# Form units of the FFN input product: fifth tiles of two forms in one ring slot, sums in two portions, an earlier store of x, T4's product behind UA

## What is computed

```
x = x + 0.5 * swiglu_ffn(rmsnorm(x, ffn1_norm), ffn1_w_in, ffn1_w_out)
...
x = x + mixed @ w_out
x = x + 0.5 * swiglu_ffn(rmsnorm(x, ffn2_norm), ffn2_w_in, ffn2_w_out)

def swiglu_ffn(x, w_in, w_out):
    gate, up = jnp.split(x @ w_in, 2, axis=-1)
    return (jax.nn.silu(gate) * up) @ w_out
```

## Time and profile before

| what | us |
|---|---|
| median of 3 runs | 1813.66 (1813.22 to 1813.73) |
| the profiled execution | 1813.04 |
| its span, first to last instruction | 1811.2 |
| PE busy in it | 1759.3 |
| VectorE busy | 1467.6 |
| ScalarE busy | 1113.4 |
| one unit of width 512 (264.79 to 308.38) | 43.59 |

### The profile page before, as it was taken

How to read it: one execution, slowest core, us unless ns; L and a number is a source line. 1 busy time by engine, 2 the same in 40 slices (tenths; PEclk the granted TensorE clock), 3 DMA queues, 4 the chain that set the end, 5 groups by cost and what they waited for, 6 DMA issues and landing times.

```text
span 1811.2 us, 21336 instructions
## 1 busy us (share of the span) xinstructions
PE 1759.3 (97%) x7976; PEld 1449.1 (80%) x7976; DVE 1467.6 (81%) x1729; ACT 1113.4 (61%) x1461; POOL 100.1 (6%) x117
## 2 busy tenths in 40 slices
PE   9999999999999999999999999799999999999999
PEld 7777777777988888888888888677777777987887
DVE  7788888888999998575665555688888888899998
ACT  7566666666676666554454445466666666666664
POOL 0100000100000001100000000100000000000000
PEclk9999999999999999999999999899999999999999
DMA  9988888887754656555555445898888887765662
GB/s 380 299 259 260 250 253 255 249 244 195 281 194 160 239 209 202 184 183 180 163 182 167 163 163 209 296 258 246 253 259 259 248 259 226 220 224 196 227 225 96
DMA packets 169190, 408.30 MB, mean 225 GB/s; under 512 B 9112, under 2 KB 18352, under 8 KB 163584
## 3 DMA queue, kind: packets, MB, share of 16 engines
q1 hardware_dynamic: 154208, 342.03, 54.2%
q0 software_dynamic: 13760, 62.94, 15.9%
q10 hardware_dynamic: 1120, 1.97, 0.3%
HBM read 351.57 MB, written 5.79 MB: 197 GB/s over the span
## 4 chain that ended last, share of the span: by engine, by line
PE 76%; DVE 13%; issue 4%; DMA 3%; ACT 3%; SPq 1%; POOL 0%; ACTq 0%; DVEq 0%
PE bank L626 6%; PE bank L628 6%; PE bank L627 6%; DVE wlo L1300 6%; PE bank L685 5%; PE bank L687 5%; PE bank L686 5%; PE bank L757 5%; PE bank L759 5%; PE bank L758 5%; PE bank L669 5%; PE bank L670 5%; PE bank L671 5%; PE bank L783 3%; PE bank L785 3%
## 5 line engine op out<-in xcount | busy, mean ns | idle before, releaser
L1300 DVE TENSOR_TENSOR wlo<-raw,whi 128x1024 fp32r<-128x1024 f32 (+1 forms) x506 | 608.7, 1208 | 238.7 <-ACT whi L953 234.7
L953 ACT ACTIVATE whi<-raw 128x1024 fp32r<-128x1024 f32 (+1 forms) x506 | 530.0, 1049 | 340.0 <-PE bank L628 183.9
L685 PE MATMUL bank<-whi,xs 128*128 128x512 f32 (+1 forms) x608 | 239.2, 393 | 16.6 <-DVE wlo L1300 15.3
L687 PE MATMUL bank<-whi,xs 128*128 128x512 f32 (+1 forms) x608 | 234.7, 386 | 0.0
L686 PE MATMUL bank<-wlo,xs 128*128 128x512 f32 (+1 forms) x608 | 234.6, 386 | 0.0
L953 ACT ACTIVATE whi<-tsum 128x1024 fp32r<-128x1024 f32 (+1 forms) x120 | 120.4, 1034 | 72.8 <-DVE tmini L1467 38.3
L757 PE MATMUL bank<-whi,aw_hi 128*128 128x512 f32 x420 | 164.5, 392 | 0.0
L669 PE MATMUL bank<-whi,xs 128*128 128x512 f32 (+1 forms) x380 | 148.0, 390 | 16.9 <-DVE wlo L1300 16.9
L759 PE MATMUL bank<-whi,aw_lo 128*128 128x512 f32 x420 | 163.6, 389 | 0.0
L758 PE MATMUL bank<-wlo,aw_hi 128*128 128x512 f32 x420 | 163.4, 389 | 0.0
L626 PE MATMUL bank<-whi,xs 128*128 128x512 f32 x384 | 155.1, 404 | 0.4 <-DVE wlo L1300 0.4
(11 more groups left out here) (217 smaller groups left out, 3085.5 us busy)
## 6 DMA issues: line engine op xcount, KB each, us to landing
raw<-ffn_w_in SPq DMA_DIRECT2D x86, 1024.0 KB, 5.1
raw<-ffn_w_out SPq DMA_DIRECT2D x84, 1024.0 KB, 6.6
raw<-w_in SPq DMA_DIRECT2D x48, 1024.0 KB, 5.0
raw<-ffn_w_in SPq DMA_DIRECT2D x75, 512.0 KB, 4.8
tsum<-raw POOLq DMA_DIRECT2D x36, 1024.0 KB, 6.9
minis<-ffn_w_in SPq DMA_DIRECT2D x72, 256.0 KB, 5.2
last_plain<-ffn_w_in SPq DMA_DIRECT2D x36, 512.0 KB, 5.2
raw<-w_out SPq DMA_DIRECT2D x16, 1024.0 KB, 4.9
```

Of the source, the lines that this page charges most:

```text
L685: mm(banks[b][:, 0:w], xs[:, k + i, 0, tok], hi, start=starts[b] and k + i == 0, stop=False, skip_group_check=True)
L687: last = mm(banks[b][:, 0:w], xs[:, k + i, 1, tok], hi, start=False, stop=k + i == last_k, skip_group_check=True)
L953: A(whi[:, h % SLOTS, 0:n_el], src, ACT.Copy).then_inc(weights_hi, 1)
L1300: V.tensor_tensor(wlo[:, h % SLOTS, 0:n_el], src, whi[:, h % SLOTS, 0:n_el].bitcast(f32), ALU.subtract).then_inc(weights_lo, 1)
```

## The change

1. *Shared slots.* The fifth tiles of two forms lie in one ring half: T1 with B11 (`T1_B11`), T2 with B21 (`T2_B21`), T3 with B22 (`T3_B22`); T4's stays alone (`T4_LAST`). A unit has 24 halves. Since the shared half stands between the two forms' other halves, the order is now T1 (2), T1_B11, B11 (2), GA, GB, B21 (2), T2 (2), T2_B21, GC, T3 (2), T3_B22, B22 (2), UA, T4 (2), T4_LAST, UB, UC.
2. *Order.* B21 stands ahead of T2, GC ahead of T3, UA ahead of T4.
3. *Sums.* `sum_t1` and `sum_t3` have two portions of 1024 columns, the second with the fifth tile. sum_t1's stand before UB and before UC, sum_t3's before GB and before B21. sums_done counts four per unit.
4. *x.* The store to x_kept stands ahead of `x_power(2)`.

PE's matmuls are the same in number and size. The diff, cut to its core:

```diff
-T1, B11, GA, GB, T2, B21, T3, GC, B22, T4, UA, UB, UC = 0, 3, 6, 7, 8, 11, 14, 17, 18, 21, 24, 25, 26
-UNIT_HALVES = 27
+T1, T1_B11, B11, GA, GB, B21, T2, T2_B21, GC, T3, T3_B22, B22, T4, T4_LAST, UA, UB, UC = (
+    0, 2, 3, 5, 6, 7, 9, 11, 12, 13, 15, 16, 19, 21, 18, 22, 23)
+UNIT_HALVES = 24
...
-                        last = (B11 + 2, T3 + 2, B22 + 2, T4, GA, GB, GC, UA, UB, UC)[i]
+                        last = (B11 + 1, T3_B22, B22 + 1, T4, GA, GB, GC, UA, UB, UC)[i]
...
-            x_power(2)
             pool.wait_ge(x_updated, 8 * 2)
             pool.dma_start(x_kept.rearrange("(b p) d -> p b d", p=P), x[:]).then_inc(x_stored, 16)
+            x_power(2)
             for j in range(1, UNITS):
-                add_piece(1, j, "B22", T1, t2_added)
-                add_piece(1, j, "B21", T2, t4_added)
+                add_piece(1, j, "B22", T1_B11, t2_added)
+                add_piece(1, j, "B21", T2_B21, t4_added)
...
+            def last_tiles(h, w, *parts):
+                pe.wait_ge(weights_lo, h + 1)
+                for i, (bank_out, stationary, start, stop) in enumerate(parts):
+                    last = tile(h, i, bank_out, stationary, 4, w, start, stop)
+                last.then_inc(weights_used, 1)
...
+                form(base + T1, Z, s1, w, True, False)
+                last_tiles(base + T1_B11, w, (Z, s1, False, True), (Y, a11, True, False))
+                form(base + B11, Y, a11, w, False, True)
                 act_turn(u, j - 1)
                 pe.wait_ge(copied, 3 * first + 1)
                 plain(base + GA, 0, (Z, X), (False, True), w, -1)
                 plain(base + GB, 2, (Z, X), (False, True), w, -1)
+                form(base + B21, V, a12, w, True, False)
                 pe.wait_ge(copied, 3 * first + 2)
+                form(base + T2, Y, s2, w, False, False)
+                last_tiles(base + T2_B21, w, (Y, s2, False, True), (V, a12, False, True))
+                plain(base + GC, 4, (Z, X), (False, False), w, FORM_K0 - 1)
                 pe.wait_ge(copied, 3 * first + 3)
+                form(base + T3, Y, s3, w, False, False)
+                last_tiles(base + T3_B22, w, (Y, s3, False, True), (Z, s4, False, False))
+                form(base + B22, Z, s4, w, False, True)
                 pe.wait_ge(w_done, first + 1)
+                plain(base + UA, 0, (V, Y), (False, False), w, -1)
+                form(base + T4, Y, a22, w, False, False)
+                last_tiles(base + T4_LAST, w, (Y, a22, False, False))
+                for i in range(2):
+                    plain(base + UB + i, 2 + 2 * i, (V, Y), (False, False), w, FORM_K0 - 1)
...
+            def split_two(h, src0, src1, w):
+                dve.wait_ge(weights_hi, h + 1)
+                V.tensor_tensor(wlo[:, h % SLOTS, 0:w], src0, whi[:, h % SLOTS, 0:w].bitcast(f32), ALU.subtract)
+                V.tensor_tensor(wlo[:, h % SLOTS, w:2 * w], src1, whi[:, h % SLOTS, w:2 * w].bitcast(f32),
+                                ALU.subtract).then_inc(weights_lo, 1)
...
+            def sum_t1(u, j, i):
                 n11, n12, w = unit_piece(u, j, "B11"), unit_piece(u, j, "B12"), UNIT_W[j]
+                if i == 0:
+                    full(n11)
+                    full(n12)
+                    if j > 1:
+                        dve.wait_ge(weights_lo, unit_half(u, j - 1) + T4_LAST + 1)
+                done = V.tensor_tensor(t_half(i, w), form_half(n12, i, w), form_half(n11, i, w), ALU.add)
+                if i:
+                    done = V.tensor_tensor(tmini[:, 0:w], form_last(n12, w), form_last(n11, w), ALU.add)
+                done.then_inc(sums_done, 1)
```

More of the change, by code:

```diff
@@ L1091, in unit @@
                 first, w2 = (UNITS - 1) * u + j - 1, 2 * w
-                def form_split(form, i, name=None):
-                    src = form_half(unit_piece(u, j, name), i, w) if name else t_half(i, w)
-                    split(base + form + i, src, form_el(i, w))
+                n11, n12, n21, n22 = (unit_piece(u, j, name) for name in ("B11", "B12", "B21", "B22"))
                 def plain_split(name, half):
@@ new lines, in unit @@
+                split_two(base + T2_B21, tmini[:, 0:w], form_last(n21, w), w)
+                plain_split("GC", GC)
+                for i in range(2):
+                    act_e.wait_ge(sums_done, 4 * first + 3 + i)
+                    split(base + T3 + i, form_half(n12, i, w), w2)
+                act_e.wait_ge(weights_used, base + T2_B21 + 1)
+                A(gset[:, s, 0, 0:w], Y[:, 0:w], ACT.Copy).then_inc(copied, 1)
+                loaded(n22)
+                split_two(base + T3_B22, form_last(n12, w), form_last(n22, w), w)
@@ L1513, in unit @@
                 first, w2 = (UNITS - 1) * u + j - 1, 2 * w
-                def form_split(form, i, name=None):
-                    src = form_half(unit_piece(u, j, name), i, w) if name else t_half(i, w)
-                    split(base + form + i, src, form_el(i, w))
+                n11, n12, n21, n22 = (unit_piece(u, j, name) for name in ("B11", "B12", "B21", "B22"))
                 def plain_split(name, half):
                     split(base + half, plain_half(unit_piece(u, j, name), w2), w2)
-                for i in range(3):
-                    form_split(T1, i)
@@ L1524, in unit @@
-                form_split(B11, 0, "B11")
+                for i in range(2):
+                    split(base + T1 + i, t_half(i, w), w2)
+                split_two(base + T1_B11, tmini[:, 0:w], form_last(n11, w), w)
+                split(base + B11, form_half(n11, 0, w), w2)
                 swiglu(u, j - 1)
-                for i in range(1, 3):
-                    form_split(B11, i, "B11")
+                split(base + B11 + 1, form_half(n11, 1, w), w2)
                 plain_split("GA", GA)
-                sum_t3(u, j)
+                sum_t3(u, j, 0)
@@ new lines, in unit @@
+                for i in range(2):
+                    split(base + T2 + i, t_half(i, w), w2)
+                split_two(base + T2_B21, tmini[:, 0:w], form_last(n21, w), w)
+                plain_split("GC", GC)
+                for i in range(2):
+                    split(base + T3 + i, form_half(n12, i, w), w2)
+                split_two(base + T3_B22, form_last(n12, w), form_last(n22, w), w)
+                for i in range(2):
+                    split(base + B22 + i, form_half(n22, i, w), w2)
```

152 lines of the change are left out of this document (68 added, 84 removed).

## The result

| | before | changed |
|---|---|---|
| median of 4 runs, us | 1813.53 (1813.22 to 1813.73) | 1765.75 (1765.19 to 1766.61) |
| ratio | | 0.9737 [0.972, 0.9754] |
| profiled execution, us | 1813.04 | 1765.33 |
| its span, us | 1811.2 | 1763.4 |

The change takes 47.7 us off the profiled execution. The forecast was 47.5 us less and 1766.1 in all. From here L numbers are lines of the changed kernel, or of the kernel that a fence is said to be of: the form products are L666 to L668 (L669 to L671 before), the plain ones L694 to L696, the low part L1323 and sum_t1 L1496 and L1498.

The account below looks back on a forecast made before the run. PE was taken to be held up by VectorE's late low parts (waits of 29.9 us in form and 15.3 us in plain products). Terms 10.9 + 1.0 + 0.4 + 18.5 + 1.1 + 10.5 + 4.1 + 1.0 = 47.5 us gave 1766.1 us, range 1757 to 1783.

Parts of the forecast that it names:

- D: Rival: T4's product waits in every unit for its accumulating DMA; at a landing of 15 us, 1830 us; chance 0.04.
- SwiGLU: Part 1, B11's second half: wanted three matmuls later, lateness 1.05 to 0.37 us; 10.9 + 1.0 + 0.4 us gained.
- Rival B: The SwiGLU wait at B11 stays because VectorE is delayed by the 0.68 us given: 1778 us; chance 0.12 with its mirror.
- sum_t1: Part 2, before UB and UC: the cut sum ends plain products' waits, UB 0.5 and UC 0.4 us in time; 18.5 + 1.1 us.
- Rival A: The sum's wait only moves to UC, if T4's start is 0.8 us later: 1777.5 us; chance 0.14.
- Store: Part 3, second FFN's start: storing x ahead of its norm's power removes PE's wait and slow clock; 10.5 us gained.
- rival C: The store, now meeting the plain unit's loads, doesn't help and 10.5 us stay: 1776.6 us; chance 0.07.
- B21 ahead of T2: Part 4, each FFN's first unit: B21 covers T2's wait for accumulating DMAs; 4.1 us gained in the first, 1.0 second.
- T4 behind UA at nothing: Part 5: T4's later DMA lands at 25.6 us, before ScalarE wants it at 27.4; priced at nothing, cover 1.8 us.
- The signs: Expected trace: about 18 B11 waits of some 0.2 us, T2 under 1, units 41.5 to 41.8 us, store at about 1105.
- rival B's mirror: The SwiGLU wait at B11 vanishes wholly, 8 us more gained: 1758 us; chance 0.12 together with rival B.

Follow-up runs that it names:

- a_sum: Changed kernel with both portions of sum_t1 ahead of UB's low part, none between UB and UC: 1793.88 us.
- a_store: Changed kernel with the store of x put back behind the norm's power: 1775.29 us.
- b_store: Kernel before, with only the store of x moved ahead of the norm's power: 1801.39 us.
- a_t4: Changed kernel with T4 put back ahead of UA on all three engines: 1776.83 us.
- b_swiglu: Kernel before, with only SwiGLU's three steps moved behind all of B11's low parts: 1816.11 us.
- b_four: Kernel before, with the store of x moved, sum_t1 and sum_t3 each in two portions and SwiGLU behind B11; no shared slots: 1766.14 us.
- a_t2: Changed kernel with T2 put back ahead of B21: 1772.26 us.
- b_sum: Kernel before, with only sum_t1 cut in two portions, ahead of UB and UC: 1794.93 us.
- a_swiglu: Changed kernel with SwiGLU's three steps behind both of B11's low parts: 1756.48 us.
- a_early: a_swiglu's kernel with T2's and T4's large accumulating DMA issued one step earlier, large and small with separate waits: 1750.72 us.
- a_swiglu_bias: a_swiglu's kernel with POOL's broadcast of the bias vectors moved behind the first unit's sums: 1758.51 us.
- a_early_bias: a_early's kernel with the broadcast of the bias vectors moved behind the first FFN's units on POOL's queue: 1750.62 us.

## Why the prediction was right, point by point

The total was right, 47.7 against 47.5 us in the profiled executions, partly by luck (see the sum below), and no rival came in full; D's mechanism came in two units. The terms:

1. *SwiGLU.* Right. The lateness at B11's second half fell from 1.05 to 0.31 (forecast 0.37), in all 16 full units; in the narrow ones the listed wait fell by 0.59, from 1.24 to 0.65, where a fall of 0.51 had been forecast. Rival B needed VectorE to lose what PE gave it; instead B11's first low part still starts 1.29 us behind T1's first matmul (263.06 and 261.77; 1.35 before), with the pair of low parts of T1_B11 ahead of it.
2. *sum_t1.* Right in the gain, and a_sum shows the cause. T4's low part starts 12.4 us before the unit's end, as placed. The slack behind it was too generous: UB is 0.27 us in time and not 0.5, UC 0.1 and not 0.4. VectorE starts the sum 0.82 us behind the start of tmini's low part (252.81 to 253.63), where I had counted 0.60. Rival A, with its 0.14, was one tenth of a microsecond away. The split itself cost nothing that shows.
3. *Store.* Right: 10.5 us forecast; the stretch between transposes that holds it is 10.5 us shorter than before, and taking it back costs 9.5 (a_store). That it would meet the plain unit's loads was rival C's premise; it did, at 11.7 us instead of 6.74, and it was done 23 us before sum_t1 began.
4. *B21 ahead of T2.* Right in direction, off in both sizes, and the errors cancel. In the first FFN PE lost 2.0 us and not 0.9: from 68.07 to 70.23 is 2.16, less 0.227, and the slow restart. I had left the landing where it was; the small DMA went out at 54.24 and landed after 13.5 us, so ScalarE began at 67.77 and not at 66.93. In the second FFN it landed in 8.9 us; I had taken the longest landing, 12.3, and the wait went altogether (1.9 gained, not 1.0). b_store, where this wait is gone with T2 ahead of B21, and a_store, where it is gone with the store late, show that either part alone removes it.
5. *T4 behind UA at nothing.* Wrong for two of the 20 units. I worked out the cover of the DMA, from 17.9 to 27.4 us, for a full unit alone. In a unit of 384 columns ScalarE wants T4 at 450.55 and the small DMA goes out at 443.18: 7.4 us, not 9.5, for a landing of 10.2. That costs the 1.42 and 1.20 listed, and T4's second half is 0.2 late too. From transposes to transposes the two last units take 36.8 and 36.6 us instead of 34.8: 3.8 us. a_t4 shows the mechanism, and that without UA it is worse. Rival D was this mechanism, but I let it decide for all 20 units or none.

*The sum again.* A full unit gained 1.98 us (43.53 to 41.55 from one B11 wait to the next), not 0.68 + 1.16 = 1.84: 16 x 0.14 = 2.2 more. The waits on the way into the two narrow units gave 0.3 more. T2 gave 1.1 less in the first FFN and 0.9 more in the second, and T4 in the narrow units took 3.8 back. That makes -1.5. Another 1.65 us came where the forecast has no term, in the second FFN's output product (1592 to 1661 in the kernel before), whose matmuls are the same: PE's weight loads there have 3.1 us of listed waits before and 0.5 after. Behind the last transposes the kernel before and the four with b_ take 221.2 to 221.9 us, the changed kernel and those made from it 219.4 to 220.6. Why is open. With it the terms come within 0.1 of the measured +0.2. So the total is closer than its terms deserve: T4's loss was made good by gains that no term had.

*The signs.* The wait list came as described, with no wait in the units' plain products; a full unit took 41.55 us, and the granted clock was 1.00 in the second FFN's first unit. The store went out at 1087.56 and not at about 1105, as everything ahead of it came some 18 us earlier too. Two signs went against the forecast: T2 in the first FFN waited 1.77 us and not under 1, and ScalarE waited for tmini before T4 in the two narrow units, which was the sign named for D.

*The step that left something out* was the treatment of SwiGLU as fixed: the same change with SwiGLU behind both halves of B11 would have been 9 us faster, which rival B's mirror (1758) had priced at 8 without naming the edit.

## What to carry to other kernels

Where three engines go through one ring in a fixed order, an engine that is nearly full carries its backlog along: moving one step only moves the wait (b_swiglu), until the next undivided lump is cut too (b_four). List for every product how early its low part is, cut whatever stands between two wanted halves into pieces of one low part's size (1.14 us here), and then move steps.

Work out the narrow last unit by itself, since the covers shrink with its width and a transfer's time need not (the small DMA landed in 10.2 and 9.9 us there, 8.6 in the median). Give each part of a transfer its own trigger and its own wait, so that the large part goes as early as its data allow.

## What the runs showed of the hardware

The cost of a long wait isn't its length. Behind waits of 3.0 to 8.1 us the granted clock was 0.50 to 0.74 over the next 4 to 6 us: 0.57 behind 3.22 and 0.59 behind 8.08, 0.58 behind 3.00 (b_swiglu), 0.50 behind 3.53 (a_t2), 0.50 and 0.74 behind 3.34 and 4.50 (a_t4). Behind 1.77 us in the changed kernel it was 1.00, so T2's wait, 1.4 us shorter, gave back 3.1 us. In between the length doesn't decide: the clock was 1.00 behind 1.85 (b_swiglu) and 2.21 (a_t4), but 0.64 behind 1.88 (b_sum), 0.71 behind 1.92 (a_sum) and 0.57 behind 2.34 (a_t2). A wait of some 2 us has to be priced for both cases.

The same accumulating DMA of a fifth tile (256 KB, behind its 1 MB companion) landed in 6.1 to 13.5 us in the changed kernel, 8.6 in the median. In the first unit, with a broadcast and loads beside it, it took 12.9 us (a_swiglu) and 14.2 (a_early); with the broadcast moved away and the loads left, 9.7 (a_swiglu_bias) and 8.9 (a_early_bias). So its time is best taken from the row of its own place.
